# One more chunk of each FFN by seven half-width products, with the sums and low parts it needs taken earlier and in another order

## What is computed

```python
def swiglu(x, w_gu, w_down):
    a, b = jnp.split(x @ w_gu, 2, axis=-1)     # w_gu: 1024 x 5632
    return (jax.nn.silu(a) * b) @ w_down       # w_down: 2816 x 1024
```

## Time and profile before

| | us |
|---|---|
| median of 3 runs (lowest, highest) | 2054.97 (2053.71, 2055.51) |
| the profiled execution | 2053.88 |
| span of its profile | 2052.2 |
| TensorE busy | 2022.4 (99%) |
| VectorE, ScalarE, GpSimd busy | 1349.7, 813.0, 737.5 |

### The profile page before, as it was taken

How to read it: one execution, slowest core, us unless ns; L and a number is a source line. 1 busy time by engine, 2 the same in 40 slices (tenths; PEclk the granted TensorE clock), 3 DMA queues, 4 the chain that set the end, 5 groups by cost and what they waited for, 6 DMA issues and landing times.

```text
span 2052.2 us, 34350 instructions
## 1 busy us (share of the span) xinstructions
PE 2022.4 (99%) x13509; PEld 1856.7 (90%) x13509; DVE 1349.7 (66%) x1842; ACT 813.0 (40%) x1163; POOL 737.5 (36%) x443
## 2 busy tenths in 40 slices
PE   9999999999999999999999999999999899999998
PEld 9899998988988989999898999889887699999887
DVE  4477774554435767777466788646899786766645
ACT  5433451253423344444234444423453434434422
POOL 1488720043312247770014777001100324776000
PEclk9999999999999999999999999999999999999999
DMA  7544322332211234443232545223544322332232
GB/s 250 185 144 157 129 87 92 110 105 77 68 32 62 93 114 151 156 162 101 94 106 93 164 144 170 99 95 113 175 133 160 103 71 92 104 102 92 88 102 89
DMA packets 229497, 239.13 MB, mean 117 GB/s; under 512 B 5983, under 2 KB 222173, under 8 KB 227612
## 3 DMA queue, kind: packets, MB, share of 16 engines
q1 hardware_dynamic: 228764, 235.68, 35.3%
q10 hardware_dynamic: 640, 2.16, 0.3%
HBM read 215.80 MB, written 22.02 MB: 116 GB/s over the span
## 4 chain that ended last, share of the span: by engine, by line
PE 83%; DVE 6%; POOL 5%; issue 3%; ACT 2%; DMA 0%; SPq 0%; DVEq 0%; POOLq 0%; ACTq 0%
PE bank L1756 11%; PE bank L1757 11%; PE bank L1758 11%; PE bank L1885 10%; PE bank L1887 10%; PE bank L1886 10%; PE bank L1767 3%; PE bank L1768 3%; PE bank L1769 3%; DVE u L1665 2%; POOL xlo L531 1%; ACT whi L661 1%; POOL s L553 1%; POOL diag_tmp L585 1%; PE bank L1839 1%
## 5 line engine op out<-in xcount | busy, mean ns | idle before, releaser
L661 ACT CAST whi<-raw 128x2048 fp32r<-128x2048 f32 (+2 forms) x192 | 326.3, 1701 | 881.3 <-POOL scratch L560 441.6
L1112 DVE TENSOR_TENSOR wlo<-raw,whi 128x2048 fp32r<-128x2048 f32 (+2 forms) x166 | 365.1, 2200 | 244.9 <-ACT whi L661 244.5
L537 POOL TENSOR_TENSOR tiny<-tiny 128x2 f32<-128x2 f32 (+1 forms) x13 | 9.4, 726 | 754.5 <-DVE tiny L1383 754.5
L556 POOL TENSOR_TENSOR raw<-raw 128x512 f32<-128x512 f32 x72 | 216.9, 3012 | 0.0
L1756 PE MATMUL bank<-h_hi,whi 128*128 128x512 f32 x528 | 207.1, 392 | 0.0
L1757 PE MATMUL bank<-h_lo,whi 128*128 128x512 f32 x528 | 205.5, 389 | 0.0
L1758 PE MATMUL bank<-h_hi,wlo 128*128 128x512 f32 x528 | 205.5, 389 | 0.0
L1885 PE MATMUL bank<-t_hi,whi 128*128 128x256 f32 x576 | 163.6, 284 | 5.2 <-DVE bank L1175 5.2
L1756 PE MATMUL bank<-xhi,whi 128*128 128x512 f32 x400 | 160.7, 402 | 3.3 <-DVE wlo L1112 3.3
L1887 PE MATMUL bank<-xhi,wlo 128*128 128x256 f32 x576 | 163.0, 283 | 0.0
L1885 PE MATMUL bank<-t_hi,ex_hi 128*128 128x256 f32 x576 | 163.0, 283 | 0.0
(11 more groups left out here) (351 smaller groups left out, 5868.5 us busy)
## 6 DMA issues: line engine op xcount, KB each, us to landing
raw<-in_ffn_w_gu_dram SPq DMA_DIRECT2D x88, 1024.0 KB, 4.9
raw<-in_ffn_w_down_dram SPq DMA_DIRECT2D x32, 896.0 KB, 5.1
raw<-in_ffn_w_down_dram SPq DMA_DIRECT2D x32, 512.0 KB, 3.4
raw<-in_gla_w_in_dram SPq DMA_DIRECT2D x14, 1024.0 KB, 5.1
early_raw<-in_conv_w_in_dram SPq DMA_DIRECT2D x18, 512.0 KB, 4.2
lo_scratch<-early_lo SPq DMA_DIRECT2D x18, 512.0 KB, 3.2
diag_scratch<-diag_tmp SPq DMA_DIRECT2D x8, 1024.0 KB, 8.7
raw<-in_conv_w_in_dram SPq DMA_DIRECT2D x16, 512.0 KB, 5.4
```

What stands on the lines that cost most here:

```text
L556: nc.gpsimd.tensor_tensor(a21, a21, a11, ALU.add).then_inc(w_sum, 1)
L661: nc.scalar.copy(whi[:, s, 0:kc, 0:width], raw[:, s, 0:kc, 0:width]).then_inc(hi_ready, 1)
L1112: nc.vector.tensor_tensor(wlo[:, s, 0:kc, 0:width], raw[:, s, 0:kc, 0:width], whi[:, s, 0:kc, 0:width].bitcast(F32), ALU.subtract).then_in ...
```

## The change

Four things change.

1. The up chunk of pair 1 goes through `seven_products` in all four FFNs. In front of it TensorE writes bank 6 (in FFN 0 banks 6 and 7) with one matmul of 512 tokens each. GpSimd takes this chunk's sums before it waits for `t_ready`; ScalarE makes its `whi` after them.
2. The activation sums are made earlier. For FFN 1 to 3 the first waits only for four blocks of `xhi` and the second for eight blocks of `xhi` and four of `xlo`. ScalarE rounds two of them before the next gate chunk's `whi` (in FFN 0 after the wait for `kv_stored`) and two after the SiLUs. VectorE takes all four low parts right behind the `wlo` of pair 1's gate chunk.
3. The third weight sum, `s4`, is rounded and subtracted ahead of the other two; GpSimd's last sum waits for `s4` alone, and TensorE waits for both before its second product.
4. At the end of the convolution the last `mo_lo_part` stands ahead of the last sums, GpSimd's first low part waits for the diagonal of 1/sigma, and three `c_lo` blocks are taken between the last `scale` steps.

```diff
-PER_FFN = 2 * FK - 2 * PLAIN
-SUMMED = FK - 2 * PLAIN
+FIRST_SUM = 3
+SUMMED = FK - FIRST_SUM
+SILU_PER_FFN, MUL_PER_FFN = 2 * FK - 4, 2 * FK - 2
...
 def weight_sums(f, i, s):
-                    pool.wait_ge(ex_lo_ready, 2 * q - 3)
+                    pool.wait_ge(ex_lo_ready, 2 * q - 2)
...
-                    pool.wait_ge(ex_lo_ready, 2 * q)
+                    pool.wait_ge(ex_lo_ready, 2 * q - 1)
...
             def all_weight_sums(f):
+                weight_sums(f, 1, 1)
                 pool.wait_ge(t_ready, 4 * f + 4)
...
             for i in range(PLAIN):
                 diagonal(i)
+            weight_sums(0, 1, 1)
             pool.wait_ge(t_ready, 4)
...
             rsqrt(LN_CONV, 0)
+            pool.wait_ge(rstd_diag, UNIT[LN_CONV] + 1)
             split_lo(CONV_OUT_N + 2, 0, B_K, after_dve=True)
...
+                nc.scalar.copy(ex_hi[s][:, 2], s4).then_inc(ex_hi_ready, 1)
                 nc.scalar.copy(ex_hi[s][:, 0:2], s12[s][:, :, :, :]).then_inc(ex_hi_ready, 1)
-                nc.scalar.copy(ex_hi[s][:, 2], s4).then_inc(ex_hi_ready, 1)
...
+                if isinstance(i, int) and i == 0:
+                    if f == 0:
+                        act.wait_ge(kv_stored, 64)
+                    x_sums_hi(f, (0, 1))
                 act.wait_ge(w_used, FFN_N[f] + 2 * i + 1)
                 next_hi(f, i, 0)
...
+                    if f:
+                        dve.wait_ge(x_hi_ready, base + (DK if j else DK // 2))
+                        dve.wait_ge(x_ready, base + (0, DK // 2, DK, DK)[j])
+                    else:
+                        dve.wait_ge(x_ready, DK)
...
+            def plain_pair(f):
+                n = FFN_N[f]
+                x_sums(f)
+                split_lo(n + 2, 0)
+                x_sums_lo(f)
...
+                split_lo(n + 3, 1)
+                extra_lo(f, 1, 1)
...
                 for k in range(DK - ahead, DK):
                     scale(k)
+                    if ln == LN_CONV and k >= 5:
+                        c_low((k - 5,))
...
+            mo_lo_part(1, 3)
             dve.wait_ge(taps_done, 6 * WIDTH)
...
-            mo_lo_part(1, 3)
             add_squares(2)
...
-                pe.wait_ge(ex_lo_ready, 2 * q + 1)
+                pe.wait_ge(ex_lo_ready, 2 * q + 2)
                 product(r5, *weight_sum(0), *x_sum(0), True).then_inc(part_mm, 1)
...
             def ffn(f, between=None):
                 plain_pair(f, 0, between)
-                for i in range(1, PLAIN):
-                    plain_pair(f, i)
+                plain_pair(f, 1)
+                for b in (6, 7) if f == 0 else (6,):
+                    nc.tensor.matmul(bank[b][:, :], xhi[:, 0, 0:P], xhi[:, 0, :], start=True, stop=True)
                 pe.wait_ge(t_ready, 4 * f + 4)
+                seven_products(f, 1, 1)
```

More of the change, by code:

```diff
@@ L137, with silu_by, mul_by @@
 RES_PER = 2
-def gated_by(f, i):
-    return PER_FFN * f + (2 * i if isinstance(i, int) and i < PLAIN else 4 * i - 2 * PLAIN)
+def silu_by(f, i):
+    return SILU_PER_FFN * f + (2 * i if isinstance(i, int) and i < PLAIN else 4 * i - 4)
+def mul_by(f, i):
+    return MUL_PER_FFN * f + (0 if isinstance(i, int) and i == 0 else 4 * i - 2)
 def summed(f, i, g):
-    return SUMMED * f - 2 * PLAIN + 2 * i + g
+    return SUMMED * f - FIRST_SUM + 2 * i + g
 def build(nc, a, out):
@@ L679, in h_hi_parts, with x_sums_hi @@
                     nc.scalar.copy(h_hi[:, k, :], hid[:, k, :]).then_inc(h_hi_done, 1)
+            def x_sums_hi(f, js):
+                for j in js:
+                    act.wait_ge(t_sum, 4 * f + j + 1)
+                    nc.scalar.copy(t_hi[:, j], T_SUM[j][0]).then_inc(t_hi_ready, 1)
             def ffn_pair(f, i):
@@ L695, in ffn_pair @@
                         nc.scalar.activation(act_out[t], bank[t][:, :], ACT.Silu).then_inc(silu_done, 1)
+                if isinstance(i, int) and i == 0:
+                    x_sums_hi(f, (2, 3))
                 if sums_next:
@@ L702, in ffn_pair @@
                 next_hi(f, i, 1)
-                if sums_next:
+                if isinstance(i, int) and i == 0:
+                    act.wait_ge(t_ready, 4 * f + 4)
+                    extra_hi(f, 1, 1)
+                elif sums_next:
                     extra_hi(f, i + 1, 1)
[L705 to L710, removed]
                 if f in (1, 2) and (not isinstance(i, int) or 0 < i <= EARLY):
@@ L1177, in summed_pair @@
             def summed_pair(f, i):
-                n, last = FFN_N[f] + 2 * i, isinstance(i, int)
+                n = FFN_N[f] + 2 * i
                 for step in range(3):
@@ L1189, in summed_pair, with summed_up @@
                                             ALU.subtract).then_inc(early_done, 1)
+                summed_up(f, i)
+            def summed_up(f, i):
+                n, last = FFN_N[f] + 2 * i, isinstance(i, int) and i == FK // 2 - 1
                 for step in range(3):
@@ L1202, in summed_pair @@
                     tok = slice(m % 2 * HALF, m % 2 * HALF + HALF)
[L1203 removed]
+                    pieces = 2 if isinstance(i, int) and i < PLAIN else 4
+                    dve.wait_ge(silu_done, silu_by(f, i) + m * pieces // 4 + 1)
                     nc.vector.tensor_tensor(hid[:, bass.ds(2 * i + m // 2, 1), tok],
@@ L1403, in last_rows, with c_low @@
                                                    op0=ALU.mult, op1=ALU.add).then_inc(fin_dve, 1)
+            def c_low(ks):
+                for k in ks:
+                    dve.wait_ge(x_hi_ready, x_base(LN_CONV, 0) + k + 1)
+                    dve.wait_ge(affine_done, x_base(LN_CONV, 0) - DK + k + 1)
+                    nc.vector.tensor_tensor(c_lo[:, k, :], u[:, k, :], c_hi[:, k, :].bitcast(F32),
+                                            ALU.subtract).then_inc(x_ready, 1)
             def norm(ln, h):
@@ L1436, in norm @@
                     scale(k)
+                    if ln == LN_CONV and k >= 5:
+                        c_low((k - 5,))
             def ffn(f):
-                for i in range(PLAIN):
-                    plain_pair(f, i)
-                dve.wait_ge(mul_done, gated_by(f, PLAIN))
+                plain_pair(f)
+                summed_up(f, 1)
+                dve.wait_ge(mul_done, mul_by(f, PLAIN))
                 with dve.Fori(PLAIN, FK // 2 - 1) as i:
@@ L1733, in _ @@
             norm(LN_CONV, 0)
[L1735 to L1742, removed]
+            c_low((3,))
             dve.wait_ge(x_ready, x_base(LN_CONV, 0) + 1)
```

49 lines of the change are left out of this document (19 added, 30 removed).

## The result

The changed kernel takes 2065.1 us (median of 4 runs, 2063.78 to 2067.53) against 2054.3 for the kernel before in the same job: a ratio of 1.0055, 95% interval 1.0043 to 1.0067. That is slower by 10.8 us, near the forecast of 2067.5. The profiled execution took 2064.42 us, with a span of 2062.6, 10.4 us above that of before.

What follows compares the result with a forecast made beforehand. TensorE, busy 99% of the span, was taken as the bound, except in FFN 0's pairs. Terms 7.5 + 10.1 - 4.4 = +13.2 us on the profiled 2053.88 gave 2067.1, stated as 2067.5; range 2054 to 2075.

Steps and rivals of the forecast that it cites:

- The likeliest case: Whole kernel: the forecast itself, slower, 2067.5 us with its own range of 2061 to 2073; chance 0.57.
- The turn-taking: VectorE additions or subtractions with two SBUF inputs and GpSimd additions never run together; a GpSimd addition takes 3.35, alone 1.29.
- VectorE keeps its place: Rival: GpSimd's sums get in only when VectorE has nothing waiting; +3 us, 2057; chance 0.17.
- the faster rival: Rival: the activation sums don't block; -13 to -15 us, 2040; chance 0.14.
- The signs named in advance: For FFN 1 to 3: activation sums spread over more than 10 us, stall of about 2 before pair 1's gate chunk.
- Part 2: Into FFN 1, 2 and 3: sums of VectorE and GpSimd block each other; +3.4 us each, +10.1 in three.
- the first terms: In FFN 1 to 3: TensorE 2 us late at `xlo`, gate chunk of pair 1 starting 2.9 us later.
- Part 3: FFN 0: new sums and low parts join the shared queue, TensorE stalls near 94 us; +7.5 us.
- the 0 for the order of `s4`: FFN 0: the new order moves a wait and takes no work out of the turn; 0 us.
- the diagonals set the pace: FFN 0: until the eighth diagonal is built, turns of VectorE and GpSimd, not TensorE, pace the pairs, 21.6 us each.
- Part 4: End of the convolution: earlier statistics, L1424 freed of GpSimd, first `c_lo` at 1621.4 instead of 1626.12; -4.4 us.
- The clock: Rival: stalls of 2 to 4 us before a chunk drop the clock to 1.2 GHz; +20 us, 2074; chance 0.12.

Runs made afterwards that it cites:

- the additions: Kernel before with four GpSimd additions of constants that nothing needs, behind the `xlo` of FFN 1 to 3: 2069.92 us against 2054.73, ratio 1.0077.
- the memsets: Kernel before with nine GpSimd memsets, which read nothing in SBUF, behind the `xlo` of FFN 1 to 3: 2054.45 us, ratio 1.0001.
- point 3 alone: Kernel before with only the order of `s4` changed, rounded and subtracted first, waits adapted: 2054.35 us against 2054.90, ratio 0.9998.
- the last run: Kernel before with the convolution's new end, `wlo` between activation sums, FFN 0's diagonals built and stored by ScalarE, no SyncE wait: 2039.87 us against 2053.63.
- the sums late: Changed kernel with the activation sums of FFN 1 to 3 waiting as before, none among the `xlo`: 2074.32 us against 2054.90 for before.
- GpSimd's wait alone: Kernel before with one line added at the convolution's end, GpSimd's wait for the diagonal of 1/sigma: 2050.68 us, ratio 0.9984.

## Why the prediction was right

The likeliest case came about, by its own steps; the sum is +10.4 us on the profiled execution, not +13.2. The number is closer than its working: by the prediction's own sum the median should have come out at 2054.97 + 13.2 = 2068.2, not 2067.5. And for FFN 1 to 3 it was luck in part that 10.1 was forecast and 9.6 came, since a size that was too large and a loss that had no term nearly cancelled.

- **The turn-taking** is shown, by the additions and the memsets. The rival that VectorE keeps its place and the faster rival fall with them: four additions that nothing needs cost 4.6 to 4.9 us in each FFN, nine memsets -0.2 to +0.4. The signs named in advance came: `xlo` 7.92 us (8), the four activation sums from 739.47 to 749.62 (over 10 us), a stall of 1.72 (about 2). Among the `xlo` the first sum kept its 1.23 us and `xlo` paid.
- **Part 2, FFN 1 to 3: mechanism right, the first terms too large, and one term missing.** At the start of pair 2 the changed kernel is 2.1, 2.3 and 2.4 us late, not 3.4. Of the predicted 2.0 us at the `xlo`, 1.4 came (1.05 of it as idle time in the three waits); the gate chunk started 2.0 late, not 2.9 (stall 1.72, not 2.2); the wait at the low parts was 0.43, not 1.1. Behind that, FFN 1 lost another 2.0, FFN 2 0.7 and FFN 3 nothing, which I had not priced.
- **That loss** stands at the second product, released by step 0 of `combine`:

```profile
809.09 0.38 PE L1913 MATMUL bank<-t_hi,ex_hi 128*128 128x256 f32 x1 [0.69 <-DVE bank L1185]
```

```profile
806.38 2.31 DVE L1206 TENSOR_TENSOR early_lo<-early_raw,early_hi 128x1024 fp32r<-128x1024 f32 x1
808.62 0.42 DVE L1185 TENSOR_SCALAR bank<-bank 128x256 f32<-128x256 f32 x1
```

  In front of that step stands a low part for the convolution's weights (L1206), 2.31 us here and 1.21 in before; FFN 3 has none. GpSimd's last sum, which used to start behind both low parts of the sums, now starts beside the second and takes its turn ahead of L1206. That order comes from point 3 of the change: with point 3 alone this low part takes 2.31 us as well. But point 3 alone lost only 0.2 us in FFN 1. Why it costs more in the changed kernel stays open.
- **Part 3, FFN 0: +5.5 instead of +7.5.** The stall near 94 us was 3.16, not 4. The stall that was to end at 131.8 ended at 130.78, 6.5 late. The pairs then came 84.24 / 4 = 21.1 us apart, not 21.6, so 1 us was given back. The 21.6 was one pair's: over four pairs from 145.88 on, before had 21.3. The term that was mis-sized is the 0 for the order of `s4`: alone it shortens FFN 0 by 1.9 us in its trace. It takes no work out of the turn, but it lets GpSimd's last sum begin sooner. That the diagonals set the pace is shown by the last run: without them on GpSimd a pair takes 20.2 us.
- **Part 4: -5.0 instead of -4.4**, with each stop where it was put. Set back by the 12.93 us, `by_halves` starts at 1617.97 (predicted 1618.2) and the first `c_lo` comes at 1621.28 (1621.4). From there on another 0.1 us was gained, where 0.3 had been allowed for the clock.
- **The clock** was halved after the 3.16 and the 2.94 us stall, for about 3.4 us each, and not after the 1.72 us stalls of FFN 1 to 3. So that rival's 1.7 us in each FFN did not come. It came with the sums late, where the stalls are 5.05 us.

## What to carry to other kernels

Where two engines take turns, add up the instructions of both over a stretch, as if they were one engine, before giving either more to do: if the sum is near the stretch, a small saving on TensorE can be paid back several times over, as 0.6 us was here by 2.4 to 4.1 us in each of three FFNs. First look for orders within one engine's list and for work that a third engine can take. When work moves to another engine, go through every queue that waits for its result, a load queue above all: the moved diagonals cost 73 us through one wait between the loads, and shortened FFN 0 by 6.5 with that wait gone.

## What was unexpected of the hardware

- Nine GpSimd memsets (5.22 us in all) leave VectorE's two-input instructions at full pace, while four additions cost them 3 us. So here work that only writes could be put into such a stretch free (ratio 1.0001).
- ScalarE's 16 scaled copies of a diagonal (4.80 us) and GpSimd's two broadcast multiplications (3.76) do the same work; the longer one is the cheaper here, since it stands outside the turn-taking of GpSimd and VectorE: with it FFN 0 is 6.5 us shorter.
- TensorE's granted clock stayed at 1.00 (2.4 GHz) behind the stalls of 1.72 us and fell to 0.50 (1.2 GHz) behind those of 2.94, 3.16, 4.06 and 5.05 us. So a stall made 2 to 3 us longer can cost more than its own length, as the late sums did. But the length of one stall doesn't decide it: at the first `c_lo` the clock fell behind 1.84 us with GpSimd's wait alone, behind 1.58 us with the memsets and 1.60 with the additions, and stayed at 1.00 behind 1.44 us in before. Each such fall, for 3.4 us, went with 1.6 us more from that `c_lo` to the end of the stretch, 10.8 us instead of 9.2.
